# Starting a gated recurrence two weight slots earlier, and norming two latents together, in a two-block transformer kernel on Trainium2

## The reference, cut to what matters

```
def hybrid_layer(x, ...):
    h = rms_norm(x) * (1 + sc_m) + sh_m
    proj = h @ w_in
    x_lru, q_down, kv_down, k_rope, gate_a, gate_b = split(proj)
    y_a = rg_lru(causal_depthwise_conv(x_lru), ...)          # eight blocks of 128 channels
    y_b = mla(q_down, kv_down, k_rope, ...)
    y = sigmoid(gate_a) * y_a + sigmoid(gate_b) * y_b
    x = x + g_m * (y @ w_out)
    ... gated MLP ...

def rg_lru(x, ...):                                          # per block of 128 channels
    r = sigmoid(x @ w_a + b_a);  i = sigmoid(x @ w_x + b_x)
    log_a = -8 * r * softplus(-a_param)
    a, mult = exp(log_a), sqrt(-expm1(2 * log_a))            # 0 and 1 where the position is 0
    h[t] = a[t] * h[t-1] + x[t] * i[t] * mult[t]

def mla(q_down, kv_down, k_rope, ...):
    q = rms_norm(q_down, q_norm_g) @ w_uq                    # q_down: 256 channels
    kv = rms_norm(kv_down, kv_norm_g) @ w_ukv                # kv_down: 128 channels
    rope on parts of q and on k_rope; causal softmax attention, 8 heads
```

## Time and profile before

| | us |
|---|---|
| median of 3 runs | 2979.19 |
| lowest and highest | 2973.77 and 2980.08 |
| the profiled execution | 2977.21 |
| its span, first to last instruction | 2975.4 |
| PE busy in the span | 2705.4 (91%) |
| DVE busy | 1767.2 (59%) |
| ACT busy | 951.4 (32%) |

### The profile page before, as it was taken

How to read it: one execution, slowest core, us unless ns; L and a number is a source line. 1 busy time by engine, 2 the same in 40 slices (tenths; PEclk the granted TensorE clock), 3 DMA queues, 4 the chain that set the end, 5 groups by cost and what they waited for, 6 DMA issues and landing times. The chain is left out here.

```text
span 2975.4 us, 27966 instructions
## 1 busy us (share of the span) xinstructions
PE 2705.4 (91%) x11102; PEld 1986.4 (67%) x11102; DVE 1767.2 (59%) x2476; ACT 951.4 (32%) x1236; POOL 0.2 (0%) x4
## 2 busy tenths in 40 slices
PE   6898675999999949999999799999999979999997
PEld 2695231367888727888877347788887734778886
DVE  1644543078766587566678767655568876653334
ACT  1322321134223224223346333322233633332222
POOL 0000000000000000000000000000000000000000
PEclk8897775999999979999999899999999989999999
DMA  5121111214544314544322001445432200122322
GB/s 227 43 86 43 43 64 47 102 61 152 183 161 172 137 45 147 191 159 167 139 92 90 22 24 68 152 169 189 165 136 85 85 32 32 57 87 93 109 80 85
DMA packets 58234, 313.98 MB, mean 106 GB/s; under 512 B 6039, under 2 KB 11543, under 8 KB 37240
## 3 DMA queue, kind: packets, MB, share of 16 engines
q1 hardware_dynamic: 58104, 312.19, 29.3%
HBM read 310.07 MB, written 2.10 MB: 105 GB/s over the span
## 5 line engine op out<-in xcount | busy, mean ns | idle before, releaser
L438 PE MATMUL psum<-x_hi,w_hi 128*128 128x512 f32 x1968 | 785.1, 399 | 10.7 <-DVE squares L1181 10.7
L439 PE MATMUL psum<-x_lo,w_hi 128*128 128x512 f32 x1968 | 769.3, 391 | 0.0
L440 PE MATMUL psum<-x_hi,w_lo 128*128 128x512 f32 x1968 | 768.9, 391 | 0.0
L1232 DVE TENSOR_TENSOR w_lo<-w_raw,w_hi 128x2048 fp32r<-128x2048 f32 (+1 forms) x192 | 418.5, 2181 | 299.3 <-ACT w_hi L842 297.4
L842 ACT ACTIVATE w_hi<-w_raw 128x2048 fp32r<-128x2048 f32 (+1 forms) x192 | 350.6, 1827 | 543.2 <-DMA w_raw<-in_w 542.5
L438 PEld LDWEIGHTS psum<-x_hi,w_hi 128*128 128x128 f32 x1968 | 371.1, 189 | 105.3 <-issue 20.0
L440 PEld LDWEIGHTS psum<-x_hi,w_lo 128*128 128x128 f32 x1968 | 371.1, 189 | 78.8
L439 PEld LDWEIGHTS psum<-x_lo,w_hi 128*128 128x128 f32 x1968 | 371.2, 189 | 77.8 <-issue 4.8
L438 PE MATMUL psum<-hidden_hi,w_hi 128*128 128x512 f32 x912 | 358.6, 393 | 0.0
L439 PE MATMUL psum<-hidden_lo,w_hi 128*128 128x512 f32 x912 | 355.1, 389 | 0.0
L440 PE MATMUL psum<-hidden_hi,w_lo 128*128 128x512 f32 x912 | 354.9, 389 | 0.0
(11 more groups left out here) (349 smaller groups left out, 2823.6 us busy)
## 6 DMA issues: line engine op xcount, KB each, us to landing
w_raw<-in_w SPq DMA_DIRECT2D x160, 1024.0 KB, 4.9
ada_w<-in_ada SPq DMA_DIRECT2D x96, 768.0 KB, 6.3
w_raw<-in_w SPq DMA_DIRECT2D x32, 704.0 KB, 4.0
w_raw<-in_ada SPq DMA_DIRECT2D x20, 768.0 KB, 5.0
big<-in_ada SPq DMA_DIRECT2D x12, 768.0 KB, 12.2
extra<-in_w_uq SPq DMA_DIRECT2D x8, 384.0 KB, 3.2
residual<-in_xT SPq DMA_DIRECT2D x1, 2048.0 KB, 14.7
small<-in_lru_w SPq DMA_DIRECT2D x2, 1024.0 KB, 6.8
```

Of the source, the lines that this page charges most:

```text
L438: mm(o, w_h, x_h, start=first, stop=False)
L439: mm(o, w_h, x_l, start=False, stop=False)
L440: return mm(o, w_l, x_h, start=False, stop=last)
L1232: v.tensor_tensor(wl[:, r, 0:n], raw[:, r, 0:n], wh[:, r, 0:n].bitcast(f32), ALU.subtract).then_inc(w_split.sem, 1)
```

## The change

Four things, in both hybrid layers.

1. Block t of the recurrence goes with slot n = t instead of n = t + 2: its two matmuls on PE stand ahead of slot t, ACT's gates and DVE's `lru_a(t)` and `lru_b(t-1)` as well.
2. Even and odd blocks have sets of buffers of their own: PSUM banks 4, 5 or 6, 7, and `big` 28 or the first tile of `staging` for the tanh. The waits are now for the block two before, not one before. ACT no longer waits for its own last instruction at two places.
3. The norms of both latents are done together. ACT squares the three tiles at slot 7 (the latent tiles are evacuated with slot 5), PE sums at slot 8 ahead of its 48 matmuls (three matmuls of plain float32), ACT takes both roots at slot 8, and DVE does both reciprocals, the products and the rotation behind `lru_b(7)`, with none of the waits in between. The kv latent has its own tile, `latent2`, the second of `staging`.
4. DVE's splits of slots n+2 come behind the recurrence's instructions of slot n instead of ahead of them; those of the first two `out2` slots come behind the rotation; and the wait for the last evacuation of `gate_a` now stands just ahead of the eight products with `big` 16 to 23.

```
 PE
                 for n, (st, s) in enumerate(gates):
-                    if n >= 2:
-                        t = n - 2
-                        eng.wait_ge(S("conv_ready").sem, S("conv_ready").next(me))
-                        eng.wait_ge(S("gates_read").sem, max(0, 8 * l + t))
-                        mm(B(4), LRU_W[:, t, :], big[:, t, :], start=True, stop=True)
-                        me.count(mm(B(5), LRU_W[:, 8 + t, :], big[:, t, :], ...).then_inc(S("gates_out").sem, 1), ...)
+                    if n < KD:
+                        t, bank = n, 4 + 2 * (n % 2)
+                        eng.wait_ge(S("conv_ready").sem, KD * l + t + 1)
+                        if t >= 2:
+                            eng.wait_ge(S("gates_read").sem, KD * l + t - 1)
+                        mm(B(bank), LRU_W[:, t, :], big[:, t, :], start=True, stop=True)
+                        mm(B(bank + 1), LRU_W[:, 8 + t, :], big[:, t, :], ...).then_inc(S("gates_out").sem, 1)
+                    if n == KD:
+                        eng.wait_ge(S("latents_squared").sem, l + 1)
+                        for k in range(2):
+                            mm(B(4), ones[:], sq[:, k, :], start=k == 0, stop=k == 1)
+                        mm(B(5), ones[:], latent2, start=True, stop=True).then_inc(S("latents_summed").sem, 1)
                     slot(st, s, xh, xl)
-                square_sums(2)
-                square_sums(1)
 ACT
-                        if n >= 2:
-                            lru_gates(n - 2)
-                        if n >= 3:
-                            lru_root(n - 3)
+                        if n < KD:
+                            lru_gates(n)
+                        if 1 <= n <= KD:
+                            lru_root(n - 1)
+                        if n == KD - 1:
+                            latent_squares()
+                        if n == KD:
+                            latent_roots()
                         where = place_of[st.name]
                         evacuate(st, sl, ...)
-                lru_root(7)
-                eng.wait_ge(evacuated.sem, hybrid[l][4].evac0)
-                norm_root([big[:, 24 + k, :] for k in range(2)], T, 2 * P, eps6)
-                norm_root([big[:, 26, :]], T, P, eps6)
 DVE
-                split_ahead(*gates[0])
-                split_ahead(*gates[1])
-                lru_a(0)
-                for t in range(KD):
-                    split_ahead(*gates[t + 2])
-                    if t + 1 < KD:
-                        lru_a(t + 1)
-                    lru_b(t)
-                eng.wait_ge(evacuated.sem, hybrid[l][4].evac0)
-                inverse_root()
+                for n, gate in enumerate(gates):
+                    if n < KD:
+                        lru_a(n)
+                    if 1 <= n <= KD:
+                        lru_b(n - 1)
+                    if n < KD:
+                        split_ahead(*gate)
+                eng.wait_ge(S("latent_roots").sem, l + 1)
...
+                split_ahead(*gates[KD])
+                split_ahead(*gates[KD + 1])
...
+                eng.wait_ge(evacuated.sem, hybrid[l][4].evac0)
                 for t in range(KD):
                     me.count(v.tensor_tensor(big[:, t, :], big[:, t, :], big[:, 16 + t, :], ALU.mult)...
```

54 lines of the change are left out of this document (33 added, 21 removed).

## The result

| | before | after |
|---|---|---|
| median, lowest and highest, us | 2977.05 (2973.77 to 2980.08) | 2931.16 (2928.21 to 2934.24) |
| ratio, 95% interval | 1 | 0.9846 [0.9829, 0.9863] |
| profiled execution and its span, us | 2977.21, 2975.4 | 2934.24, 2932.4 |

The kernel is 45.9 us faster by the medians and 43.0 by the two spans. The forecast was 2933.8, with a range from 2922 to 2945. The median before is now that of four runs; the forecast started from three of them, whose median was 2979.19.

A forecast was written before the change was run, and what follows sets the result against it. PE, busy 91% of the span, was taken as the bound, with a hole before attention in both hybrid layers. Saving 22.4 and 22.0 us from 2977.2 gives 2932.8; the middle between that and 2934.8 is 2933.8, range 2922 to 2945.

The forecast's parts named there:

- The hole: From E to the first score: 1.55 us to the first projection plus 9.63 onward; before, 36.17 and 35.71 us.
- E: Start of the last of slot 9's 48 matmuls on PE, from which the time to the first score is counted.
- the term for the clock: First projection to first score: the clock, fallen in the hole, had cost 2.1 and 1.4 us; it would stay up.
- The sums: Three float32 matmuls ahead of slot 8, six records of 0.43, cost 2.58 us in PE's full stream.
- The covers: DVE and ACT ready ahead of PE: 7.6 us to spare at the first projection, 2.9 and 0.3 at products and q's rotation.
- The prediction's sign: A check in the profile after: DVE's rotation done 7 us ahead of the end of slot 9.
- B: Recurrence on DVE and ACT fails to keep pace with the slots, `latents_ready` 7.5 us late per layer: 2949; chance 0.04.
- C: The recurrence loop holds up PE's slots through late splits, making the kernel slower: 2987; chance 0.02.
- D: First projection still waits for a late signal and the hole stays: 2975 to 2979; chance 0.03.
- A: Attention's entrance becomes DVE's, products late through the second `out2` load or split: 2940 with 3 us lost per layer; chance 0.08.
- Attention's own clock: First score to `out2`, 122.83 and 118.16 us before, taken as unchanged, with 4.7 us either way.
- rival E: The clock draws quite differently in the attentions, beyond 4.7 us: 2921.5 to 2943; chance 0.10.

The follow-up runs named there:

- hole_filled: The kernel before, with fourteen matmuls that nobody reads added on PE in the hole behind slot 9; median 2970.91 us, ratio 0.9978 to before.
- slack_two: The changed kernel with two more reciprocals on DVE ahead of the rotation, in both layers; median 2945.62 us, ratio 0.9891 to before.
- latents_only: The kernel before with only the changed treatment of the latents' norms, recurrence still from slot 2 on; median 2972.94 us, ratio 0.9990 to before.
- after_again: The changed kernel run once more without an edit; median 2934.19 us, ratio 0.9855 to before.
- `slack` kernels: The changed kernel with two or four more reciprocals on DVE ahead of the rotation; medians 2945.62 and 2959.72 us, ratios 0.9891 and 0.9945 to before.

## Why the prediction was right, point by point

**The hole.** Predicted from E to the first score 1.55 + 9.63 = 11.18, measured 1.61 + 9.59 = 11.20 in both layers. The hand-over after ACT's evacuation took 0.06 more than I gave it, and the way to the score, which I took from the pieces of before at full clock, 0.04 less. `hole_filled` shows that the term for the clock in it, 2.1 and 1.4 us, was the right one.

**The sums.** Predicted 2.58 in a full stream, measured 125.31 - 122.70 = 2.61.

**The covers.** The rotation was over at 1639.1, for a first projection at 1646.8: 7.7 to spare, 7.6 predicted. The split of slot 2 was done 7.3 ahead (7.4). DVE waited for ACT's tanh from block 4 on (block 5 predicted). The products waited 2.80 for the evacuation (2.9), the rotation of q 0.35 for ACT's third copy (0.3). `slack_two` confirmed the first of these: 6.7 us of extra work did not delay the first projection. It confirmed the second only roughly: with 6.8 of work and 3.2 of cover I expected the first score 3.6 later, and it came 2.76 later. What I had left out is a further 0.3 ahead of the second split and 0.54 between the end of q's rotation (1655.86) and the first score (1656.40), where PE is still at the last projections. The prediction's sign that the rotation is done 7 us ahead of the end of slot 9 did not fit its own sum, 1640.1 against 1646.15 for E; measured it is 6.1 ahead of E.

**The rivals.** B, C and D did not happen: the way from the first gate matmul to E took 125.3 us in every kernel that has the change's order there, and PE's waits hold no entry of a slot for its split. A did not happen either, but its price was wrong, and that is the one step which failed on the chip. "From 3.2 us of delay each microsecond costs one in each layer" leaves out that PE, once idle ahead of the attention, was granted less for its first piece: behind 2.6 us of idle time it took 6.5 and 7.9 us more. `slack_two`, with the first score 2.76 late, came at 2945.6; the working of A would give 2940 or less for it, and the range's end lay at 2945. `latents_only` shows the same at its worst.

**Attention's own clock.** I took it as before, with 4.7 to either side, and it came 0.8 longer. That it came so near is luck: in `after_again` the changed kernel had attentions 2.0 shorter than the kernel before. The reason given for the 4.7 was right in kind: of the 4.7 between the layers of before, 5.3 are the draws of the last two pieces, less 0.6 elsewhere. The Trainium skill, "TensorE: Matmul & The Clock Gate", Part 1 (What's actually happening), which the prediction cited for rival E, says that the watching is not aligned with the kernel. The runs agree with that for equal work: 121.14 and 117.83 for `after_again`, 121.13 and 120.65 for the same kernel in `after`. What the runs add is that the draws take few sizes and stand behind particular idle times, and that filling these moves them. So they are a property of the kernel in part, which my rival E did not have.

**The level.** Of the 2.0 us between the profiled execution and the median I took one half. Against the profiled execution of after (2934.24) the sum 2932.8 is 1.4 short, of which 0.8 are the attentions; against the median it is 1.6 too high, and the forecast with its half of the 2.0 is 2.6 too high. With the fourth run the median before stands at 2977.05, so that the 2.0 was an accident of three runs.

**What stays open.** Why the first piece falls to 0.72 behind 2.6 us of idle time in all four layers of the two `slack` kernels, while 1.33 us later on is followed by a lower clock in 39 of 52, is described here and not explained. And the way before the first hybrid layer differs by up to 5.5 us between profiled executions of kernels that are the same there (E of the first layer at 1642.2 to 1647.7), which no run here was made for.

## What to carry to other kernels

When a hole on the busiest engine is a chain over the others, look for all the links on it: here the norms alone, taken out of the hole, pushed the recurrence behind them, and the recurrence alone, started early, left two norms in series. Either half came out near nothing, both together at 46 us. Price a microsecond of idle time on PE by what is seen behind it as well: here 2.6 us ahead of the first score were 9.1 and 10.5 by the end of the next piece, and 5 to 6 in the kernel. And where PE waits a microsecond for another engine in a stretch that it is nearly full in, a dead matmul in the gap can be worth more than the gap: 13.8 us here for ten of them in two layers.

## What the runs showed of the hardware that was not expected

- The granted clock behind a short idle time: 17.97 us of PE work without a gap became 24.45 and 25.90 behind 2.6 us of idle time, at 0.72 and 0.67 of full speed, and 17.98 again when the idle time was filled.
- The attention's time is not spread: of its nine pieces some have one size and the others two or a few (17.9 or 19.5; 11.3 or 14.4), and which one comes differs between the two layers and between executions of one kernel (121.14 and 117.83 in one).
- A plain f32 matmul of 128x512 is two records of 0.43 each, 0.86 us for one instruction of the program. Six of them took 5.31.
- Work added to the busiest engine made it busy for less time: 22.38 us with 58 records, 19.32 with 67.
